# Expert weights in one ring of nine places, over three pairs per turn of the loop; the last combine in fp32; the first weight lead of block 2 ahead of the copies of x2

## The reference

```python
def hierarchical_moe(h, w_rg, b_rg, w_re, b_re, w1, w3, w2):   # 32 experts
    # each token: the best of 4 groups, in it the best 2 of 8 experts
    ...
    def expert_block(args):
        xb, e = args
        hid = jax.nn.silu(xb @ w1[e]) * (xb @ w3[e])    # 1024 -> 512, twice
        return hid @ w2[e]                              # 512 -> 1024
    ...                                                 # weighted sum over a token's experts

x = x + ga2 * hierarchical_moe(modulate(rms_norm(x, g_norm2), sh2, sc2), ...)   # end of block 1
h = rms_norm_2(x, norm_mix_g)                                                   # block 2
z = h @ w_in_2            # chunks of 512 columns; the first is called fq
```

## Time and profile before

| | |
|---|---|
| median of 3 runs | 1162.46 us (1160.97 to 1162.48) |
| profiled execution, span from first to last instruction | 1159.7 us |
| the profiled execution's own time | not given apart from its span |
| PE busy | 1120.9 us (97%) |
| DVE, ACT, POOL busy | 485.4, 415.9, 184.4 us |
| bytes by DMA | 331.68 MB, mean 286 GB/s |
| mean granted clock of PE | 0.996 |

### The profile page before, as it was taken

The page is one execution under the profiler, slowest core; times in us unless marked ns, Lnnn a source line. Parts: engine busy times, 40 slices in busy tenths (PEclk is TensorE's granted clock), DMA queues, the critical chain, the costliest instruction groups (busy, mean ns, idle before and its releaser), DMA issues.

```text
span 1159.7 us, 15465 instructions
## 1 busy us (share of the span) xinstructions
PE 1120.9 (97%) x5860; PEld 751.4 (65%) x5860; DVE 485.4 (42%) x968; ACT 415.9 (36%) x618; POOL 184.4 (16%) x79
## 2 busy tenths in 40 slices
PE   6899999999999999999989998999999999999998
PEld 3689777864444444444434444988878888888876
DVE  4686344662222222222212214689574653333136
ACT  4543643331111111211111115575465354344234
POOL 0303232000000000000000001200314064442522
PEclk9999999999999999999999998999999999999999
DMA  9968668789799999999999998443424366555451
GB/s 354 374 218 297 230 250 314 286 326 403 327 386 421 423 422 421 423 422 421 423 420 422 421 421 316 146 147 144 146 80 162 133 216 205 158 181 200 163 181 37
DMA packets 96393, 331.68 MB, mean 286 GB/s; under 512 B 8097, under 2 KB 30866, under 8 KB 70738
## 3 DMA queue, kind: packets, MB, share of 16 engines
q1 hardware_dynamic: 96064, 330.58, 73.6%
q0 software_dynamic: 80, 0.26, 0.1%
q10 hardware_dynamic: 194, 0.06, 0.0%
HBM read 329.84 MB, written 1.05 MB: 285 GB/s over the span
## 4 chain that ended last, share of the span: by engine, by line
PE 75%; DMA 17%; DVE 3%; ACT 2%; SPq 1%; issue 1%; DVEq 0%; ACTq 0%
DMA ring<-in_w 16%; PE ps L882 14%; PE ps L883 14%; PE ps L884 14%; PE ps L1256 13%; PE ps L1298 5%; PE ps L1228 1%; PE ps L1229 1%; DMA ring<-in_w_ada 1%; PE ps L957 1%; PE ps L1409 1%; DVE ring_r L2082 1%; ACT ring_r L1621 1%; SPq L752 1%; PE ps L1312 1%
## 5 line engine op out<-in xcount | busy, mean ns | idle before, releaser
L845 POOL TENSOR_TENSOR ring_r<-ring,ring_r 128x1024 fp32r<-128x1024 f32 x66 | 172.0, 2628 | 710.1 <-ACT ring_r L1621 710.0
L1256 PE MATMUL ps<-ring,arena 128*64 128x512 f32 x1008 | 225.9, 596 | 8.6 <-DMA ring<-in_w 7.5
L883 PE MATMUL ps<-ring_r,hl_r 128*128 128x512 f32 x528 | 209.7, 397 | 0.0
L882 PE MATMUL ps<-ring_r,hl_r 128*128 128x512 f32 x480 | 195.8, 408 | 6.6 <-DVE hr_r L2174 2.7
L884 PE MATMUL ps<-ring_r,hr_r 128*128 128x512 f32 x480 | 190.7, 397 | 0.0
L1621 ACT ACTIVATE ring_r<-ring 128x2048 fp32r<-128x2048 f32 x88 | 163.6, 1908 | 49.9 <-PE ps L884 44.9
L1256 PEld LDWEIGHTS ps<-ring,arena 128*64 128x64 f32 x1008 | 69.5, 137 | 148.8 <-issue 127.5
L2082 DVE TENSOR_TENSOR ring_r<-ring,ring_r 128x2048 fp32r<-128x2048 f32 x55 | 129.5, 2365 | 78.8 <-ACT ring_r L1621 78.5
L883 PEld LDWEIGHTS ps<-ring_r,hl_r 128*128 128x128 f32 x528 | 100.0, 189 | 21.8
L882 PEld LDWEIGHTS ps<-ring_r,hl_r 128*128 128x128 f32 x480 | 90.8, 189 | 33.5 <-issue 9.2
L884 PEld LDWEIGHTS ps<-ring_r,hr_r 128*128 128x128 f32 x480 | 90.8, 189 | 22.0
(11 more groups left out here) (371 smaller groups left out, 1618.6 us busy)
## 6 DMA issues: line engine op xcount, KB each, us to landing
ring<-in_w SPq DMA_DIRECT2D x91, 2048.0 KB, 21.5
ring<-in_w_in SPq DMA_DIRECT2D x20, 2048.0 KB, 10.8
ring<-in_w_ada SPq DMA_DIRECT2D x16, 1024.0 KB, 9.7
ring<-in_w_ffn_gate SPq DMA_DIRECT2D x11, 1024.0 KB, 5.4
ring<-in_w_ffn_up SPq DMA_DIRECT2D x11, 1024.0 KB, 8.0
ring<-in_w_ffn_down SPq DMA_DIRECT2D x5, 2048.0 KB, 7.9
ring<-in_w_ada SPq DMA_DIRECT2D x4, 2048.0 KB, 7.9
ring<-in_w_o SPq DMA_DIRECT2D x2, 2048.0 KB, 8.4
```

Source lines behind the costliest of these rows:

```text
L845: nc.gpsimd.tensor_tensor(rest[:, a:b], w[:, a:b], lead[:, a:b].bitcast(F32), ALU.subtract).then_inc(sem("w_rest_b"), 1)
L882: mm(o, lhsT=a_lead, rhs=b_lead, start=start, stop=False, skip_group_check=True)
L883: mm(o, lhsT=a_lead, rhs=b_rest, start=False, stop=False, skip_group_check=True)
L1256: last = mm(H[slots_of(e), :], lhsT=xs[:, k, slots_of(e)], rhs=w, start=k == 0, stop=k == KD - 1)
```

## The change

The six blocks of a pair no longer have a place each. The blocks of all pairs are numbered r = 0 to 95 in the order of their use, and go in turn to nine places, `HOMES`: the six slots and three places beside the ring, which are kept for the whole stage (two pieces of 1 MB each, one per expert: in `gates`; in the arena and `uy`; in `spp` and `x`). Block r waits until block r - 9 has been read. Nine places and six blocks meet again after 18 blocks, so SP and PE loops now have a body of three pairs. w2's first half has a semaphore of its own, `moe_w2_used`, when its products of both column halves are issued.

The last turn's `combine` becomes `last_combine`: fp32 products of `ST` and `ys`, no lead and rest. ACT and DVE make the lead and rest of fq before the copies of x2. POOL zeroes `scT` after fq's rest and the last w2. The lead of fq waits for w3 of pair 14, not of pair 15, as slot 5 is last used by block 87.

```diff
-        early_w2 = [gates_flat[:, 0:2 * D], gates_flat[:, 2 * D:4 * D], part(14, 8), uy[:, 0:2 * D]]
-        early_w1 = [flat(x[:, :, :], "p t d -> p (t d)"), spp[:, 0:2 * D]]
+        beside = [(gates_flat[:, 0:2 * D], gates_flat[:, 2 * D:4 * D]), (part(14, 8), uy[:, 0:2 * D]),
+                  (spp[:, 0:2 * D], flat(x[:, :, :], "p t d -> p (t d)"))]
...
-        MOE_USED = ("w1_used", "w1_used", "w3_used", "w3_used", "ys0_done", "ys1_done")
+        MOE_USED = ("w1_used", "w1_used", "w3_used", "w3_used", "w2_used", "ys1_done")
+        HOMES = (4, 3, 0, 6, 7, 1, 5, 2, 8)
+        N_HOMES = len(HOMES)
+        def home(r):
+            return HOMES[r % N_HOMES]
+        def landed_at(r, g):
+            slot, each = home(r), 16 if home(r) < SLOTS else 32
+            return moe_base[slot] + each * (2 * g + r // N_HOMES + 1)
+        def piece(slot, e):
+            if slot < SLOTS:
+                return ring[:, slot, 2 * D * e:2 * D * (e + 1)]
+            return beside[slot - SLOTS][e]
...
-            first = {0: (sem("ada_pairs"), 1), 1: after("g1a"), 14: block_used(3, PAIRS),
+            first = {0: (sem("ada_pairs"), 1), 1: after("g1a"), 14: block_used(3, PAIRS - 1),
...
+        def piece_load(sp_, r, pair, e):
+            n, slot = r % 6, home(r)
+            src = rows_of_half(expert_w[n][bass.ds(2 * pair + e, 1)], n)
+            sp_.dma_start(piece(slot, e).unsqueeze(1), src).then_inc(block_in[slot], 16)
+        def block_load(sp_, r, pair):
+            n, slot = r % 6, home(r)
+            if slot < SLOTS:
+                src = rows_of_half(expert_w[n][bass.ds(2 * pair, 2)], n)
+                sp_.dma_start(ring[:, slot, :].rearrange("p (e r) -> p e r", e=2), src).then_inc(block_in[slot], 16)
+            else:
+                for e in range(2):
+                    piece_load(sp_, r, pair, e)
...
+            for r in range(1, 8):
+                if home(r) < SLOTS:
+                    sp_.wait_ge(*moe_free[home(r)])
+                else:
+                    sp_.wait_ge(*(small_after("mt11") if home(r) == SLOTS else after("wo01")))
+                block_load(sp_, r, r // 6)
+            sp_.wait_ge(sem("chosen_ready"), 1)
+            piece_load(sp_, 8, 1, 0)
+            sp_.wait_ge(sem("xp_rest"), 4)
+            sp_.wait_ge(sem("moe_gather0_done"), 1)
+            piece_load(sp_, 8, 1, 1)
+            def next_block(r, g):
+                was = r - N_HOMES
+                sp_.wait_ge(*block_used(was % 6, 3 * g + was // 6 + 1))
+                block_load(sp_, r, 3 * g + r // 6)
+            for r in range(N_HOMES, 18):
+                next_block(r, 0)
...
-            with sp_.Fori(3, PAIRS) as i:
+            with sp_.Fori(1, PAIRS // 3) as g:
+                for r in range(18):
+                    next_block(r, g)
+            for r in range(6):
+                next_block(r, PAIRS // 3)
...
-            pool.wait_ge(sem("moe_ys1_done"), 3)
-            nc.gpsimd.memset(scT, 0.0).then_inc(sem("scores_zeroed"), 1)
             for m in range(M["fq"], M["pproj"]):
                 rest_weights(m)
+                if m == M["fq"]:
+                    pool.wait_ge(sem("moe_ys1_done"), PAIRS)
+                    nc.gpsimd.memset(scT, 0.0).then_inc(sem("scores_zeroed"), 1)
...
+            def last_combine(i, done):
+                for half in range(2):
+                    pe.wait_ge(sem("moe_ys_scaled"), 2 * i + 2 * done + half + 1)
+                    for t in range(TT):
+                        mm(dense.bank(f"moe{2 * t + half}"), lhsT=ST[:, t * P:(t + 1) * P].bitcast(F32),
+                           rhs=ys[:, half * COL:(half + 1) * COL], start=False, stop=True,
+                           skip_group_check=True).then_inc(sem("moe_combined"), 1)
...
-            turn(0, 0, 0, 1)
-            turn(1, 0, 0)
-            turn(2, 0, 0, 2)
-            with pe.Fori(3, PAIRS - LATE_TURNS) as i:
-                turn(i, 0, 0)
+            for j in range(3):
+                turn(j, (0, j), 0)
+            GROUP = PAIRS // 3
+            with pe.Fori(1, GROUP - 1) as g:
+                for j in range(3):
+                    turn(3 * g + j, (g, j), 0)
             def late_turns():
-                with pe.Fori(PAIRS - LATE_TURNS, PAIRS - 1) as i:
-                    turn(i, 0, 0)
-                last_turn(PAIRS - 1, 0, 0)
+                for j in range(3):
+                    turn(3 * (GROUP - 1) + j, (GROUP - 1, j), 0)
+                last_turn(PAIRS - 1, (GROUP, 0), 0)
...
+            lead_weights(M["fq"])
             for t in range(TT):
                 act_.wait_ge(sem("moe_combined"), 4 * PAIRS - 3 + t)
                 af(x[:, t, 0:COL], dense.bank(f"moe{2 * t}"), ACT.Copy).then_inc(sem("x2_left"), 1)
-            lead_weights(M["fq"])
...
+            rest_weights(M["fq"])
             for t in range(TT):
                 dve.wait_ge(sem("moe_combined"), 4 * PAIRS - 1 + t)
                 v.tensor_copy(x[:, t, COL:], dense.bank(f"moe{2 * t + 1}")).then_inc(sem("x2_right"), 1)
-            rest_weights(M["fq"])
```

More of the change, by code:

```diff
@@ L636, in two_blocks @@
         chunk_in = [sem(f"chunk_in{s}") for s in range(SLOTS)]
-        spare_in = [sem(f"spare_in{s}") for s in range(SLOTS)]
+        beside_in = [sem(f"beside_in{s}") for s in range(len(beside))]
+        block_in = chunk_in + beside_in
+        beside_n = [32 * sum(home(b) == SLOTS + s for b in range(BLOCKS)) for s in range(len(beside))]
+        spare_in = beside_in + [sem(f"spare_in{s}") for s in range(len(beside), SLOTS)]
+        spare_base = beside_n + [0] * (SLOTS - len(beside))
         M = {name: m for m, name in enumerate(split_chunks)}
@@ L784, in _ @@
                     sp_.dma_start(cst[:, C_FIRST:], consts[:, C_FIRST:]).then_inc(sem("cst_in"), 16)
[L785 to L799, removed]
-            sp_.wait_ge(sem("moe_ys1_done"), 1)
-            for e in range(2):
-                early_w2_load(sp_, 2, e)
-            for n in (1, 2, 3):
-                sp_.wait_ge(*block_used(n, 2))
-                expert_load(sp_, n, 2, chunk_in)
+            for r in range(1, 8):
[4 more added lines that the diff above has]
+                block_load(sp_, r, r // 6)
@@ L807, in _ @@
             more = sp_.value_load(flag[0:1, 0:1], min_val=0, max_val=1)
-            with sp_.Fori(3, PAIRS) as i:
-                for n in range(6):
-                    sp_.wait_ge(*block_used(n, i))
-                    expert_load(sp_, n, i, chunk_in)
-            with sp_.If(more > 0):
-                for n in range(6):
-                    sp_.wait_ge(*block_used(n, PAIRS))
-                    expert_load(sp_, n, 0, spare_in)
+            with sp_.Fori(1, PAIRS // 3) as g:
+                for r in range(18):
+                    next_block(r, g)
@@ L817, in _ @@
+            for r in range(6):
+                next_block(r, PAIRS // 3)
+            with sp_.If(more > 0):
+                sp_.wait_ge(sem("moe_ys1_done"), PAIRS)
+                for n in range(6):
+                    spare_load(sp_, n, 0)
                 with sp_.Fori(1, PAIRS * EXTRA_ROUNDS) as i:
@@ L1297, in middle @@
                             for e in range(2):
-                                last = mm(Y[slots_of(e), :], lhsT=hidT[:, f, slots_of(e)],
-                                          rhs=w2_rows(e, f, half, early),
+                                at = (f % 2) * D + half * COL
+                                last = mm(Y[slots_of(e), :], lhsT=hidT[:, f, slots_of(e)], rhs=piece(slot, e)[:, at:at + COL],
                                           start=f == 0, stop=f == FT - 1)
@@ L1302, in middle @@
                             last.then_inc(sem(f"moe_ys{half}_done"), 1)
+                        elif half == 1:
+                            last.then_inc(sem("moe_w2_used"), 1)
             def combine(i, done):
@@ L1799, in one_pair @@
                     af(hidT, HA.rearrange("p (f c) -> p f c", c=P), ACT.Copy).then_inc(sem("moe_hidT_ready"), 1)
-                    if more_pairs:
-                        tokens_out(i + done + 2)
+                    if not more_pairs:
+                        return
+                    tokens_out(i + done + 2)
                     for half in range(2):
@@ L2424, in one_pair @@
                                                ALU.mult).then_inc(sem("moe_ys_scaled"), 1)
-                        dve.wait_ge(sem("moe_ys_lead"), 2 * i + 2 * done + half + 1)
+                        if not more_pairs:
+                            continue
+                        dve.wait_ge(sem("moe_ys_lead"), 2 * (i + done + (0 if done == 0 else -1)) + half + 1)
                         v.tensor_tensor(ys_r[:, cols_], ys[:, cols_], ys_l[:, cols_].bitcast(F32),
```

109 lines of the change are left out of this document (46 added, 63 removed).

## The result

The changed kernel takes **1148.99 us** (median of four runs, 1147.94 to 1150.35); the kernel before, on the same chip, 1162.47 (1160.97 to 1163.38). The ratio is 0.9889, with a 95% interval of 0.9873 to 0.9906. The profiled execution spans 1146.1 us, where 1159.7 was before: 13.6 less. The forecast was 1149.0.

What follows compares the result with a forecast made beforehand. Expert-block transfers, starved early by places bound to kinds, bound the stage, with PE's pace close behind; 12.5 us from the landing plus 1.0 from the order took 1159.7 to 1146.2, plus 2.8 gives 1149.0 us, range 1146 to 1155.

Steps and rivals of the forecast that it cites:

- The rate and the pockets: Expert stage: transfers at 422 GB/s, starved before 345 us; the ring regains 10.3 us, last block landing at 691.8.
- Block 13's margin: Early ring: tightest block must be out by 279.3 us and can be at 278.4, margin 0.9 us.
- Rival C: Ring: some release comes late each round, pockets stay, last block lands at 704.3; 1161.5 us, chance 0.04.
- PE's turns: Expert stage on PE: 27.7 us a turn; last w2 starts at 687.6 by PE, 687.8 by the transfers.
- The jumps' 3.4 us: PE's three-turn loop body: two jumps back at 1.69 us each, 3.4 in all, range 0 to 10.
- A: Rival at PE's loop jumps: two at 5 us each bind PE, end moves 6, 1155 us; chance 0.06.
- B: Rival at PE's loop jumps: instruction fetches queue behind expert blocks, 24.8 us each, 1194.6 us; chance 0.04.
- the 698.1 of the text: End of PE's last w2: 694.7 us by its own pace, 698.1 with 3.4 us for the two jumps.
- The tail: After the stage: fq lands 697.3, leads end 701.0, copies and norm-lead start 702.1, first block-2 product 703.8; gain 13.5 us.
- the 1.0 us (at most 1.7) of the new order: Tail on ACT: fq's leads ahead of the copies to x gain 1.0 us, at most 1.7.
- The clock: PE's granted clock after the tail's gaps, 0.81 in 715 to 720: kept, may go or grow by up to 2 us.
- What surrounds the span: Whole run: the runs' median lies 2.8 us above the profiled span, added to the forecast span of 1146.2.

Runs made afterwards that it cites:

- e1: Changed kernel with only the ring of nine places; last combine and order of fq's leads and copies as in the kernel before: 1149.93 us, ratio 0.9905.
- e3: Changed kernel with eight ring places instead of nine and a loop body of four pairs: 1155.05 us, ratio 0.9937.
- e5: Changed kernel with each turn's one-hot transposes on PE done five times, 14.1 us more PE work in all: 1166.32 us, ratio 1.0036; again, one run, 1165.69.
- e6: Changed kernel loading only half the bytes of 15 ring w3 blocks from block 9 on, 15.7 MB fewer: 1145.35 us, ratio 0.9845.
- e4: Changed kernel with each turn's one-hot transposes on PE done twice, 3.5 us more PE work in all: 1148.81 us, ratio 0.9879.
- e9: Changed kernel with each turn's one-hot transposes on PE done four times, 10.6 us more PE work in all: 1157.63 us, one run.
- r0: The changed kernel unaltered, measured again beside other runs, against the kernel before: 1148.81 us, ratio 0.9889.
- e7: Changed kernel with fq loaded in two halves, the first lead waiting for the first half alone: 1146.62 us, ratio 0.9861; again 1146.02, ratio 0.9863.
- e8: Against e7, the two left copies put between fq's two leads on ACT: 1145.76 us, ratio 0.9865.
- e2: Kernel before with only the tail's edits (fp32 unsplit last combine, fq's leads and difference ahead of the copies): 1160.71 us, ratio 0.9991.

## Why the prediction was right, step by step

**The rate and the pockets** held. (The reading of the slices is off by one at one end: 326 is slice 9, and slices 10 to 12 have 327 to 403. Nothing is worked out from it.) The pockets' 10.3 us are gone but for one, and 256.3 to 345 is at 415 GB/s where I reckoned with 422 behind a slow start. From block 9's landing to the last one's there are 692.7 - 263.8 = 428.9 us for 86 blocks, 4.99 each; I had 4.97. Block 9 took 7.5 instead of 8.1. The two make the 0.9 us by which the last landing missed 691.8. That the third of the blocks in two pieces costs nothing is shown only as far as that: 1.5 us in all at most. e1 shows that the ring alone brings the gain, and e3 confirms the mechanism with another number of places.

**Block 13's margin** of 0.9 us held: the window 258 to 300 has 420 GB/s and no pocket. Rival C is out.

**PE's turns.** Where w2 begins in the loop's last two turns of a body, in the first turn after the jump back, and in the last turn of all:

```profile
465.82 7.09 PE L1313 MATMUL ps<-ring,arena 128*64 128x512 f32 x32
...
493.54 3.65 PE L1313 MATMUL ps<-ring,arena 128*64 128x512 f32 x16
...
521.27 0.64 PE L1313 MATMUL ps<-arena 128*64 128x512 f32 x1
...
688.81 0.64 PE L1313 MATMUL ps<-arena 128*64 128x512 f32 x1 [0.69 <-ACT arena L1826]
```

From turn to turn it is 27.72 us (493.54 - 465.82), and with the jump between them 27.73 (521.27 - 493.54). Eight turns on, with the branch's 1.7 and 1.8 less for the last turn, w2 would start at 465.82 + 8 x 27.72 + 1.7 - 1.8 = 687.5; it starts at 688.81, of which 0.7 is L1273's wait for a ring block, 0.2 more is lost at the branch (29.63 from w2 to w2, for 27.72 + 1.7), and 0.4 in the last turn I can't place. The prediction had 687.6 by PE and 687.8 by the transfers. **The jumps' 3.4 us** was the mis-sized term here: they measured 0, the lower end of its range. In the window 412 to 591, which holds the jumps behind turns 5 and 8, no instruction was fetched; the DMA queues of that window are one row:

```profile
q1 hardware_dynamic: 10016, 75.76, 101.2%
```

while the whole run has 44 packets on q8 for instructions (40 before), 0.72 MB, some 16 KB each. So rivals A and B never came up at the jumps. Their mechanism is not absent, though: the forward branch before turn 12 does wait for a fetch under the same backlog, 1.7 us here and 7.3 in e5, so B's 24.8 us for one was too high and A's "three times the row" was in reach, at another place than A had it. Of the two rules that the prediction named from the Trainium skill (page "Runtime: NRT & Kernel Launch", section "Instruction fetch mechanics"), the trace agrees with PE's room for 2048 instructions and not with the window of two blocks: about 890 matmuls and weight loads of the body stayed without a fetch. PE's limit was then better than the 698.1 of the text, and nothing hung on it, since the room was 4.0 by the rows and about 3.5 as measured (e6, and with it e4, e5, e9).

**The tail** is where the steps erred, by 1.9 us at the first product of block 2 (705.67 for 703.8), which the clock behind it made good. fq landed at 698.1 (697.3 predicted, so 11.6 us sooner than before and not 12.5), the leads took their 3.7, the copies their 1.06, to 702.8. Here I had the norm leads start at once, as in the earlier trace rows, and that was the failed step: **the 1.0 us (at most 1.7) of the new order**. The norm leads read what PE's transposes of x give, and those read the copies. Before, the transposes had lain beside fq's leads, so the norm leads followed at once; in the new order copy, transpose and norm lead are one chain, and ACT waits for PE, 0.72 with the transposes at half clock, 0.26 at full clock (r0). So from landing to norm leads 0.4 us were gained where the prediction had 1.0 (715.61 - 709.78 = 5.8 before, 703.57 - 698.14 = 5.4 now), and the norm leads gained 12.0 for 13.5. In the old order, on the other hand, the copies cost less than I had reckoned once fq lands late: e1 is through with them 1.0 us after the landing and has its norm leads at 703.59 (the prediction had 703.8 for the old order and 702.1 for the new). The order is worth nothing that the runs can show, 5.0 to 5.4 us from landing to norm leads against 4.6.

**The clock** was kept in the sum, with up to 2 us either way, and it took about 1.5 us less behind the first product. In the kernel before, the last w2 took 8.78 us where another takes 7.09, at granted clock 0.50 in 702 to 704, and it has 0.81 again in 715 to 720, on the products of block 2 that set the time. After, the one such stretch in the tail is the window 702.20 to 705.60, granted clock 0.50 (1.2 GHz) after PE had stood 2.34 us for the copies; it lies on the transposes, 3.50 us for 2.02 before, of which part would have been waiting anyway, and the first product starts at 705.67 at full clock (2.4 GHz). In r0, e7 and e8 the tail has none, and in e7's second trace it lay on w2 (granted clock 0.50 in 691 to 693) and made the combine end 1.2 later than in the first. From the first product of block 2 to the end of the span it is 442.4 us in the kernel before's trace and 440.4 to 440.8 in all thirteen others, e2's too, which has the kernel before's pockets. Product by product, 1.5 of these 2.0 us arise in the first twelve products, at the half clock, and 0.35 at one product near the end (1131.5), for which I have no cause. So the shift up to the first product, 11.6, and the rest of the span, 2.0, add up to 13.6: a sum of 13.5 that was right with its parts at 11.6 and 2.0 instead of 13.5 and 0. That the two misses cancel is luck.

**What surrounds the span.** The prediction took 2.8 us between the span and the median. After, it is 2.9 (1148.99 - 1146.1), of which 1.8 surround the span (that execution took 1147.94) and 1.1 are its distance from the median. The total carried over. In the kernel before it is shared out much the same: its executions beside r0 have 1.8 around their spans too (1160.2 with 1158.4), which leaves 1.0 as the profiled one's distance from the median. So that the total carried over is partly luck as well.

**e5's miss** belongs here too: that PE's extra work costs what exceeds its room was right in e4 and e9, and fell short in e5 by the branch's stall of 7.3 us and the half clock behind it.

## What to carry to other kernels

When one stream of transfers sets a stage, ask how long each buffer stands empty: in this kernel, buffers bound to one kind of block stood empty at the seams, and the same bytes through one ring of nine in order of use ran with one pocket left; the last landing came 11.6 us sooner where 12.5 was reckoned. The number counts as well: one place less was one more block's time. And work added for a test can cost more than itself, here by a wait for instructions at a branch (e5). Then look at once for the next limit, here PE at 3.5 us, because it says how much more the transfers can give. And where two steps change places, follow who reads the moved one's output: the work that lay beside it may now stand behind it.

## What the runs showed of the hardware

A jump back over a body of three turns (some 890 matmuls and weight loads) cost PE nothing, and one over four turns did not either (e3). The forward branch on PE costs 1.5 to 1.9 us in eleven of the fourteen traces, 1.6 with a second gap of 1.7 in e9, and 7.3 and 7.5 in the two of the kernel with 14.1 us more work, with transfers at 419 GB/s beside it. In every trace PE goes on 2.3 to 2.7 us after a packet of 16 KB on the instruction queue starts, and the next packet starts 5.6 to 5.9 us after the first: that is what a fetch cost beside a full load of transfers. Stretches at half clock of a few us stand at different places in different executions of like kernels (in r0 behind the branch's wait, granted clock 0.57 in 596 to 600; in after, behind the same wait, 1.00 there). They move single spans by 1 to 2 us, and so no single trace can settle an edit of that size: the tail's order looked different in every one.
